# A two-block transformer kernel on one core: rotary step, scores and softmax of an attention stage reordered among three engines

## The chip, the cores and the metric

The kernel runs on one core of one Trainium2 chip. The time is device time in microseconds of one execution; lower is better. TensorE (PE) multiplies, VectorE (DVE) and ScalarE (ACT) do the elementwise work, SyncE (SP) issues the loads of the weights.

## What is computed

A sequence of 256 tokens of width 1024 in float32 passes through a first block of two layers and then a second block. The change lies in the token mixer of the second block alone. Cut to what matters there:

```python
def causal_depthwise_conv(u, w, b): ...      # 31 taps, 1024 channels

def mla_attention(q_nope, q_rope, k_nope, k_rope, v):
    sc = (einsum("bqhd,bkhd->bhqk", qn_b, k_nope)            # 128 deep
          + einsum("bqhr,bkr->bhqk", qr_b, k_rope)) * scale  # 64 deep, one key part for all 8 heads
    sc = where(causal, sc, -1e30)
    p = softmax(sc, axis=-1)
    return einsum("bhqk,bkhd->bqhd", p, v)

z = h @ w_in
u = silu(layer_norm(causal_depthwise_conv(ua * sigmoid(ub), conv_w, conv_b)))
y_a = u @ w_conv_out
q = rms_norm(q_lat) @ w_uq                # 8 heads of 128 + 64
kv = rms_norm(kv_lat) @ w_ukv             # 8 heads of 128 + 128
q_rope, k_rope = apply_rope(...), apply_rope(...)
y_b = mla_attention(q_nope, q_rope, k_nope, k_rope, v) @ w_attn_out
return (g_a * y_a + g_b * y_b) @ w_out
```

## The kernel before, in words

Each engine has a program of its own, written out by hand, and the programs meet at semaphores. Tokens are two tiles of 128 (`NT`), channels are eight tiles of 128 (`KT`).

A large matrix product is done in three: a value is held as a rounded high part (`wh`, `xh`) and a remainder (`wl`, `xl`), and PE multiplies high by high, low by high and high by low (lines 668 to 670). So each block of weights that SP has loaded into `raw` is split: ACT copies it into `wh` (line 1608), then DVE subtracts it from `raw` into `wl` (line 2300). `raw`, `wh` and `wl` have three slots each, and the blocks take them in a rotation that `make_plan` fixes. `split_hi` on ACT waits until PE has used the slot's last block (`w_used`), `split_lo` on DVE waits until ACT has written the slot (`hi_ready`). Both engines run their instructions in program order, so a split that waits holds up what stands behind it. The order of blocks at this place is `uq` 0 to 3, `ukv` 0 and 1, `attn_out` (0,0), (0,1), (1,0), (1,1), then `conv_out` and `out`. `ukv` 0 and 1 lie in slots 1 and 2, `attn_out` (0,0), (0,1), (1,0) in slots 0, 1, 2, and `attn_out` (1,1) in slot 0 again.

The stages around the change, in the order of PE's program:

- `uq` and `ukv`: the queries (`qn`), the keys (`kn`) and the values (`vt`) of eight heads; ACT takes them out of PSUM. `ukv` comes as two blocks of four heads, each first the keys, then the values.
- Rotation: DVE rotates the 64-wide parts of queries and key into `ro` (lines 3042 to 3048, semaphore `roped`). PE transposes `ro` in ten pieces (line 878 is the helper `turn`), ACT writes them to `qr`.
- Attention, one head after another (`scores`, lines 1510 and 1511, and `weigh`). For a head, PE makes the scores of two token tiles, of 128 and of 256 keys, each as a product 128 deep and one 64 deep in the upper or lower half of the rows. DVE scales and masks them (lines 3073 to 3075), takes the maxima (3079) and negates them (3081). ACT does the exponentials (2199, with the sums). DVE divides (`finish`, 3058 and 3061). PE transposes the weights, ACT copies them (`weights_T`, 2187), PE multiplies them with the values (1538 to 1540), ACT and DVE take the result apart into `xh` (`out_hi`, 2191) and `xl` (`out_lo`, 3066).
- The depthwise convolution fills the gaps of this. DVE does 217 taps of seven channel tiles (line 2971, `conv(n)` runs the next n of them), some before, some inside and the last 16 after the heads. PE does the 31 taps of the eighth tile, four for each head (`conv_taps`, line 1522), with diagonal matrices that ACT builds (`diag_taps`, line 2178) in two buffers.
- `attn_out`: four blocks, each 24 products for two token tiles. After the first of them PE makes the convolution's mean (`conv_mean`, line 1563), which needs all taps of DVE; after the second its variance (`conv_var`, line 1570). From the variance a chain through DVE and ACT (lines 3101 to 3121) makes the input of `conv_out`, the next stage of PE.

Of the kernel before, what the change touches and what calls it, by code (L numbers as in the profile page):

```python
# [21 lines left out]
ALU = mybir.AluOpType  # L22
# [41 lines left out]
MASKS = (("causal", P), ("unit", CH), ("diag_ts", CH), ("off_ts", CH), ("diag_st", CH), ("strict_st", CH), ("upto_st", CH), ("incl_st", P))  # L64
# [10 lines left out]
def constants():  # L75
# [15 lines left out]
    out = np.zeros((P, NMASK), np.float32)  # L91
    for n, v in m.items():
        out[:, MI[n]:MI[n] + v.shape[1]] = v
# [39 lines left out]
    "pe_18": (("ffn0.out", 3), ("ffn1.out", 3), ("out.t", 1), ("mlp.out", 3)),  # L133
# [64 lines left out]
    "dve_24": (("scaled", 16), ("at.max", 8)),  # L198
# [98 lines left out]
def build(nc, A, masks_d, pool_d, out):  # L297
    plan = make_plan()
    ctx = ExitStack()
    with ctx:  # L300
# [365 lines left out]
        def _(pe):  # L666
# [797 lines left out]

            for j in range(2):
# [6 lines left out]
                for i in range(4):  # L1472
                    for kt in range(2):
                        mm3(ps[:, bk + i // 2, (i % 2) * SEQ:(i % 2 + 1) * SEQ], w4[0][:, kt, i, 0:NOPE], w4[1][:, kt, i, 0:NOPE],
                            xh[:, 3 + kt, :], xl[:, 3 + kt, :], kt == 0, kt == 1)
# [5 lines left out]

            ro = W(3, 0, 1280).rearrange("p (t n) -> p t n", t=NT)
            pe.wait_ge(S("roped"), B("roped") + 2)
            pe.wait_ge(S("kn"), B("kn") + 2)
            pe.wait_ge(S("vt"), B("vt") + 2)
            for kt in range(5):
                b = 4 + kt // 2
                for t in range(NT):
                    m = turn(ps[:, b, (kt % 2) * SEQ + t * P:(kt % 2) * SEQ + (t + 1) * P], ro[:, t, kt * P:(kt + 1) * P])
                if kt in (1, 3, 4):  # L1490
                    m.then_inc(S("ro_T"), 1)
# [9 lines left out]
            pe.wait_ge(S("vt"), B("vt") + 4)  # L1501

            def scores(i):
                if i >= 2:
                    pe.wait_ge(S("at.sc"), B("at.sc") + 2 * (i - 1))
                rows = slice(64 * (i % 2), 64 * (i % 2) + 64)
# [7 lines left out]
            diags = DIAGS(W, lowr)  # L1514
# [10 lines left out]
            def weigh(i):  # L1525
# [7 lines left out]
                conv_taps(i)  # L1533
# [8 lines left out]
            scores(0)  # L1542
            for i in range(NH):
                if i + 1 < NH:
                    scores(i + 1)
                weigh(i)
# [26 lines left out]
            linear("attn_out", "at.xl", 2, free=ao_free, after={(0, 0): conv_mean, (0, 1): conv_var})  # L1573
# [20 lines left out]
        def _(act):  # L1594
# [556 lines left out]
            for j in range(2):  # L2151
                used(act, ("ukv", j))
                for b in range(2):
                    act.activation(kn[:, 4 * j + 2 * b:4 * j + 2 * b + 2, :], ps[:, UKV_BANK[j] + b, :].rearrange("p (a n) -> p a n", a=2), ACT.Copy)\
                       .then_inc(S("kn"), 1)
                vt = W3(5, NT)
                for t in range(NT):
                    act.activation(vt[:, t, j * 512:(j + 1) * 512], ps[:, UKV_BANK[j] + 2 + t, :], ACT.Copy).then_inc(S("vt"), 1)
                if j == 0:
                    split(("attn_out", 0, 0), ("attn_out", 0, 1))  # L2160
# [31 lines left out]
            for i in range(NH):  # L2192
                b = i % 2
                if i:
                    weights_T(i - 1)
# [1185 lines left out]
```

## Time and profile before

| | |
|---|---|
| median of 3 runs | 1197.58 us (1197.08 to 1199.15) |
| the profiled execution | 1196.4 us, of which its span 1194.3 us |
| PE busy | 1136.8 us (95%) |
| DVE busy | 825.4 us (69%) |
| ACT busy | 558.4 us (47%) |
| chain that ended last | PE 68%, DVE 21%, ACT 6%, issue 3%, DMA 2% |

PE is busy in nearly all of the span, so this is a kernel whose time is PE's own work and the places where PE waits or runs at the lower clock. The whole attention stage takes some 45 us of the span, from 870 to 915 us.

### The profile page before, as it was taken

Reading aid. Unit: us, or ns where it says so; the run is one execution under the profiler, and the core shown is the slowest. Engines: PE = TensorE matmul, PEld = TensorE weight load, DVE = VectorE, ACT = ScalarE, POOL = GpSimd, SP = SyncE. Lnnn points to the kernel's source line nnn. Section 1 sums busy time; section 2 is a strip of 40 time slices with the busy share of each in tenths; the row PEclk is TensorE's granted clock in tenths of the full one; section 3 lists DMA queues with packets and bytes.
Section 4 is the critical chain, followed back from the end, with each engine's and each line's share of the span. In section 5 each row is a group of like instructions: output and inputs, shape, how many; then the busy total and the mean of one; then the engine's idle time right before and its main releaser. Section 6 shows DMA issues by size and latency. Waiting matters only on the chain.

```text
span 1194.3 us, 20769 instructions
## 1 busy us (share of the span) xinstructions
PE 1136.8 (95%) x8520; PEld 959.7 (80%) x8520; DVE 825.4 (69%) x1173; ACT 558.4 (47%) x708; POOL 42.0 (4%) x48
## 2 busy tenths in 40 slices
PE   8999999999999887989999999999999999999998
PEld 7887888889688586767877787877967878999996
DVE  3555444558398476859999986998998667455554
ACT  5535643354654634344343464354464646344443
POOL 0000000000001400101111000000000000000000
PEclk9999999999999999989999999999989999999999
DMA  9385555652333110879999954464520344455532
GB/s 316 111 272 198 169 178 208 211 176 106 106 106 112 49 29 22 307 240 320 328 328 333 306 176 141 132 199 128 176 106 2 122 160 146 171 177 174 195 122 106
DMA packets 129476, 207.96 MB, mean 174 GB/s; under 512 B 11192, under 2 KB 86717, under 8 KB 129150
## 3 DMA queue, kind: packets, MB, share of 16 engines
q1 hardware_dynamic: 121716, 176.58, 44.6%
q0 software_dynamic: 6672, 27.26, 6.6%
q10 hardware_dynamic: 1018, 3.10, 0.7%
q8 instruction: 53, 0.87, 0.3%
q14 instruction: 17, 0.14, 0.0%
HBM read 204.83 MB, written 1.05 MB: 172 GB/s over the span
## 4 chain that ended last, share of the span: by engine, by line
PE 68%; DVE 21%; ACT 6%; issue 3%; DMA 2%; ACTq 0%; DVEq 0%; SPq 0%
PE ps L668 19%; PE ps L670 19%; PE ps L669 18%; DVE wl L2300 6%; DVE wide L2971 3%; PE ps L1061 2%; ACT wh L1608 2%; DVE wide L2410 2%; DMA raw<-in_ffn_w_up 1%; PE ps L745 1%; PE ps L878 1%; PE ps L974 1%; ACT wide L2199 1%; PE ps L1093 1%; PE ps L1366 1%
## 5 line engine op out<-in xcount | busy, mean ns | idle before, releaser
L2300 DVE TENSOR_TENSOR wl<-raw,wh 128x2048 fp32r<-128x2048 f32 (+3 forms) x158 | 354.2, 2248 | 157.8 <-ACT wh L1608 157.5
L668 PE MATMUL ps<-wh,xh 128*128 128x512 f32 (+4 forms) x1128 | 417.2, 370 | 12.8 <-DVE wl L2300 3.9
L670 PE MATMUL ps<-wl,xh 128*128 128x512 f32 (+4 forms) x1128 | 408.9, 363 | 0.0
L669 PE MATMUL ps<-wh,xl 128*128 128x512 f32 (+4 forms) x1128 | 408.4, 362 | 0.0
L1608 ACT ACTIVATE wh<-raw 128x2048 fp32r<-128x2048 f32 (+3 forms) x158 | 294.1, 1881 | 92.0 <-PE ps L670 79.8
L668 PEld LDWEIGHTS ps<-wh,xh 128*128 128x128 f32 x1128 | 213.9, 190 | 53.4 <-issue 12.4
L670 PEld LDWEIGHTS ps<-wl,xh 128*128 128x128 f32 x1128 | 213.5, 189 | 33.0
L669 PEld LDWEIGHTS ps<-wh,xl 128*128 128x128 f32 x1128 | 213.9, 190 | 31.5 <-issue 0.7
L668 PE MATMUL ps<-wh,gh 128*128 128x512 f32 x280 | 109.6, 391 | 1.9 <-DVE gl L2473 1.9
L669 PE MATMUL ps<-wh,gl 128*128 128x512 f32 x280 | 109.1, 390 | 0.0
L670 PE MATMUL ps<-wl,gh 128*128 128x512 f32 x280 | 109.0, 389 | 0.0
L1703 ACT ACTIVATE gh<-ps 128x512 fp32r<-128x512 f32 x20 | 12.0, 599 | 161.4 <-PE ps L745 161.4
L2971 DVE SCALAR_TENSOR_TENSOR wide<-wide,cols 128x256 f32<-128x256 f32 x210 | 86.3, 477 | 0.0
L2410 DVE SCALAR_TENSOR_TENSOR wide<-wide,small 128x256 f32<-128x256 f32 x192 | 78.4, 478 | 0.0
L668 PEld LDWEIGHTS ps<-wh,gh 128*128 128x128 f32 x280 | 52.6, 188 | 12.8 <-DVE gl L2473 2.1
L670 PEld LDWEIGHTS ps<-wl,gh 128*128 128x128 f32 x280 | 52.6, 188 | 11.1
L669 PEld LDWEIGHTS ps<-wh,gl 128*128 128x128 f32 x280 | 52.6, 188 | 10.3
L2436 DVE TENSOR_TENSOR gl<-ps,gh 128x512 fp32r<-128x512 f32 x20 | 13.8, 692 | 63.2 <-ACT gh L1703 62.3
L878 PE MATMUL ps<-masks,wide 128*128 128x128 f32 (+1 forms) x194 | 26.7, 277 | 6.4 <-DVE wide L3133 2.0
L878 PEld LDWEIGHTS ps<-masks,wide 128*128 128x128 f32 (+1 forms) x194 | 21.4, 140 | 12.5 <-issue 3.8
L2462 DVE TENSOR_TENSOR wide<-wide 128x512 f32<-128x512 f32 x16 | 11.1, 692 | 28.8 <-ACT wide L1730 28.8
L621 POOL DMA_DIRECT2D wide<-in_w_ada x24 | 21.3, 891 | 227.5 <-DVE wide L2410 163.1
(377 smaller groups left out, 1173.3 us busy)
## 6 DMA issues: line engine op xcount, KB each, us to landing
wide<-in_w_ada POOLq DMA_DIRECT2D x24, 1024.0 KB, 9.1
raw<-in_ffn_w_gate SPq DMA_DIRECT2D x44, 512.0 KB, 4.2
raw<-in_ffn_w_up SPq DMA_DIRECT2D x44, 512.0 KB, 5.3
raw<-in_ffn_w_down SPq DMA_DIRECT2D x22, 1024.0 KB, 5.1
raw<-in_w_mlp_in SPq DMA_DIRECT2D x16, 1024.0 KB, 7.0
raw<-in_w_mlp_out SPq DMA_DIRECT2D x16, 1024.0 KB, 5.2
raw<-in_w_in SPq DMA_DIRECT2D x16, 512.0 KB, 4.9
raw<-in_w_in SPq DMA_DIRECT2D x8, 1024.0 KB, 5.1
```

What stands on the lines that cost most here:

```text
L621: pool.dma_start(ada_raw[2 * (j % 2) + b], ada_src[:, :, n0:n0 + 256])\
L668: pe.matmul(o, lh, rh, start=start, stop=False)
L669: pe.matmul(o, ll, rh, start=False, stop=False)
L670: return pe.matmul(o, lh, rl, start=False, stop=stop)
L878: return pe.transpose(dst, src, masks[0:nk, 0:nk])
L1061: m = pe.matmul(bank(g, b + half)[to, at + j * w:at + (j + 1) * w], T(g, l, p, e, q), T(g, r, p, e, q, w), start=True, stop=True)
L1608: act.activation(wh[:, s, 0:width], raw[:, s, 0:width], ACT.Copy).then_inc(hi_ready[s], 1)
L1703: act.activation((xh if last else gh)[:, 0:2, :], ps[:, 6, :].rearrange("p (a n) -> p a n", a=2), ACT.Copy).then_inc(S(f + ".gh"), 1)
L2300: v.tensor_tensor(wl[:, s, 0:width], raw[:, s, 0:width], f32(wh[:, s, 0:width]), ALU.subtract).then_inc(lo_ready[s], 1)
L2410: v.scalar_tensor_tensor(out=o, in0=ada_raw[buf][:, k, :], scalar=ccol[:, k:k + 1], in1=o, op0=ALU.mult, op1=ALU.add).then_inc(S("ada_step ...
L2436: v.tensor_tensor(lo[:, 0:2, :], ps[:, 6, :].rearrange("p (a n) -> p a n", a=2), f32(hi[:, 0:2, :]), ALU.subtract)\
L2971: m = v.scalar_tensor_tensor(out=cv[:, kt, :], in0=src, scalar=w, in1=cv[:, kt, :], op0=ALU.mult, op1=ALU.add)
```

## The change

1. The rotation comes earlier. DVE no longer does nine taps ahead of the split of `ukv` 1. PE transposes the rotated parts between the keys and the values of `ukv` 1 instead of after the values, ACT writes `kn` and `qr` first and `vt` after, and loads the table of the exponential before them. ACT's first `diag_taps` stands ahead of `vt`.
2. Scores of two heads are made together: both heads' products 128 deep, then both heads' products 64 deep, one in each half of the rows, into two banks of PSUM. `weigh` of an even head issues the next pair's scores, and the taps of PE run one head ahead.
3. Scale, mask and maximum are one `tensor_tensor_reduce` for each token tile, on the negated scores: two instructions of DVE for a head in place of six. The exponential has a scale of -1.
4. DVE takes two heads per turn of its loop (`scored`, `conv(3)`, `scored`, `out_lo`, `conv(2)`, `finish`, `conv(4)`, `finish`, `conv(2)`, `out_lo`). The splits of `attn_out` (0,0), (0,1), (1,0), two of which stood ahead of the heads, close the first three turns. The split of (1,1), which stood behind the last tap, now stands ahead of the last 11 taps and of the last `out_lo`. Splits on ACT stand at the same places, save that of (1,1), which stays behind `conv_pe`.
5. `attn_out` is written out: (0,0) needs only four heads of `xl`; `conv_mean` stands in the middle of (0,1) and `conv_var` in the middle of (1,0).

```diff
+            def scores(j):
+
+                if j:
+                    pe.wait_ge(S("at.sc"), B("at.sc") + 4 * j)
                 for t in range(NT):
                     nk = P * (t + 1)
-                    o = ps[:, i % 2, t * SEQ:t * SEQ + nk]
-                    pe.matmul(o, qn[:, i, tok(t)], kn[:, i, 0:nk], start=True, stop=False)
-                    m = pe.matmul(o, qr[rows, i // 2, tok(t)], qr[rows, 4, 0:nk], start=False, stop=True)
-                m.then_inc(S("at.s"), 1)
+                    o = [ps[:, e, t * SEQ:t * SEQ + nk] for e in range(2)]
+                    for e in range(2):
+                        pe.matmul(o[e], qn[:, 2 * j + e, tok(t)], kn[:, 2 * j + e, 0:nk], start=True, stop=False)
+                    for e in range(2):
+                        rows = slice(64 * e, 64 * e + 64)
+                        m = pe.matmul(o[e], qr[rows, j, tok(t)], qr[rows, 4, 0:nk], start=False, stop=True)
+                        if t == NT - 1:
+                            m.then_inc(S("at.s"), 1)
...
-                conv_taps(i)
+                if i % 2 == 0 and i + 2 < NH:
+                    scores(i // 2 + 1)
+                if i + 1 < NH:
+                    conv_taps(i + 1)
...
-            linear("attn_out", "at.xl", 2, free=ao_free, after={(0, 0): conv_mean, (0, 1): conv_var})
+            ao_free(0)
+            for c in range(2):
+                o = [ps[:, 2 * c + t, :] for t in range(NT)]
+                s = arrive(("attn_out", c, 0))
+                if c == 0:
+                    pe.wait_ge(S("at.xl"), B("at.xl") + 4)
+                half(s, range(0, 2), o, 512, True, False)
+                if c:
+                    conv_var()
+                half(s, range(2, 4), o, 512, False, False, 2).then_inc(w_used[s], 1)
+                s = arrive(("attn_out", c, 1))
+                if c == 0:
+                    pe.wait_ge(S("at.xl"), B("at.xl") + NH)
+                half(s, range(4, 6), o, 512, False, False)
+                if c == 0:
+                    conv_mean()
+                half(s, range(6, 8), o, 512, False, True, 2).then_inc(w_used[s], 1)
...
+            for j in range(2):
+                if j == 0:
+                    used(act, ("ukv", 0))
+                else:
+                    act.activation(unused, eps, ACT.Exp)
+                    act.wait_ge(S("ukv.k"), B("ukv.k") + 1)
...
+            for i in range(0, NH, 2):
+                exps(i)
+                if i:
+                    out_hi(i - 2)
+                    weights_T(i - 1)
+                exps(i + 1)
+                diag_taps(i + 1)
+                if i:
+                    out_hi(i - 1)
+                weights_T(i)
+                if i + 2 < NH:
+                    diag_taps(i + 2)
+                    split(("attn_out",) + AO_AT[i])
+            out_hi(NH - 2)
             weights_T(NH - 1)
             out_hi(NH - 1)
             act.wait_ge(S("conv_mm"), B("conv_mm") + NH)
...
-            for name in [("uq", 3), ("ukv", 0), ("ukv", 1)]:
-                conv(9)
+            for name, n in [(("uq", 3), 9), (("ukv", 0), 9), (("ukv", 1), 0)]:
+                conv(n)
                 split(name)
...
-            split(("attn_out", 0, 0), ("attn_out", 0, 1))
-            conv(10)
+            conv(19)
...
-                v.scalar_tensor_tensor(out=pp[b][:, 0, 0:P], in0=ps[:, b, 0:P], scalar=SCALE, in1=causal, op0=ALU.mult, op1=ALU.add)
-                v.tensor_scalar(pp[b][:, 1, 0:P], ps[:, b, SEQ:SEQ + P], SCALE, None, ALU.mult).then_inc(S("at.sc"), 1)
-                v.scalar_tensor_tensor(out=pp[b][:, 1, P:SEQ], in0=ps[:, b, SEQ + P:2 * SEQ], scalar=SCALE, in1=causal, op0=ALU.mult,
-                                       op1=ALU.add).then_inc(S("at.sc"), 1)
-                v.wait_ge(S("at.sc"), B("at.sc") + 2 * (i + 1))
                 for t in range(NT):
-                    m = v.tensor_reduce(amax[:, 2 * b + t:2 * b + t + 1], pp[b][:, t, 0:P * (t + 1)], AX_X, ALU.max)
-                link(m)
-                v.tensor_scalar(amax[:, 2 * b:2 * b + 2], amax[:, 2 * b:2 * b + 2], -1.0, None, ALU.mult).then_inc(S("at.max"), 1)
+                    nk = P * (t + 1)
+                    v.tensor_tensor_reduce(out=pp[b][:, t, 0:nk], in0=ps[:, b, t * SEQ:t * SEQ + nk], in1=causal[t], scale=-SCALE, scalar=3e38,
+                                           op0=ALU.add, op1=ALU.min, accum_out=amax[:, 2 * b + t:2 * b + t + 1]).then_inc(S("at.sc"), 1)
+
+            for i in range(0, NH, 2):
+                scored(i)
+                conv(3)
+                scored(i + 1)
+                if i:
+                    out_lo(i - 2)
                 conv(2)
                 finish(i)
-                if i == 1:
-                    split(("attn_out", 1, 0))
-                conv(2 if i == 1 else 3)
+                conv(4)
+                finish(i + 1)
+                conv(2)
                 if i:
                     out_lo(i - 1)
+                if i in AO_AT:
+                    split(("attn_out",) + AO_AT[i])
+            out_lo(NH - 2)
+            split(("attn_out", 1, 1))
+            conv(3)
             out_lo(NH - 1)
             conv(len(taps))
-            split(("attn_out", 1, 1))
...
+AO_AT = {0: (0, 0), 2: (0, 1), 4: (1, 0)}
```

## Rows read from the trace of the kernel before

**Rows 1.** PE timeline, four places: start us, us, line, count, idle before.
```profile
519.06 1.33 PE L722 MATMUL ps<-masks,h 128*128 128x128 f32 x5 [5.26 <-DVE h L2393]
...
854.19 0.38 PE L668 MATMUL ps<-xh,wh 128*128 128x256 f32 x1 [1.38 <-DVE wl L2300]
...
867.05 1.25 PE L878 MATMUL ps<-masks,wide 128*128 128x128 f32 x10
870.63 0.49 PE L1510 MATMUL ps<-wide 128*128 128x128 f32 x2 [2.32 <-ACT wide L2165]
```

**Rows 2.** Windows: engines' busy us and instructions, then granted PE clock, DMA share, GB/s.
```profile
520.00:524.00 4.00, 4.00 (x13) 3.32 (x12) 2.87 (x6) 2.82 (x8) 0.00 (x0) 0.50 1.07 383
...
872.50:882.70 10.20, 9.72 (x28) 6.70 (x27) 9.45 (x30) 6.90 (x19) 0.00 (x0) 0.50 0.25 93
```

**Rows 3.** PE timeline, one head of the steady loop.
```profile
889.41 0.55 PE L878 MATMUL ps<-masks,wide 128*128 128x128 f32 x3
889.79 1.89 PE L1522 MATMUL ps<-wide 128*128 128x256 f32 x8
891.52 0.38 PE L1538 MATMUL ps<-wide 128*128 128x128 f32 x2
...
892.19 0.39 PE L1510 MATMUL ps<-wide 128*128 128x128 f32 x2
...
894.17 0.55 PE L878 MATMUL ps<-masks,wide 128*128 128x128 f32 x3
```

**Rows 4.** DVE timeline, the same head.
```profile
889.67 0.28 DVE L3073 SCALAR_TENSOR_TENSOR wide<-ps,masks 128x128 f32<-128x128 f32 x1
...
891.11 0.87 DVE L2971 SCALAR_TENSOR_TENSOR wide<-wide,cols 128x256 f32<-128x256 f32 x2
892.25 0.17 DVE L3058 RECIPROCAL small<-small 128x2 f32<-128x2 f32 x1 [0.27 <-ACT wide L2199]
...
892.92 1.27 DVE L2971 SCALAR_TENSOR_TENSOR wide<-wide,cols 128x256 f32<-128x256 f32 x3
894.11 0.41 DVE L3066 TENSOR_TENSOR xl<-ps,xh 128x256 fp32r<-128x256 f32 x1
```

**Rows 5.** DVE timeline, the same kind of instruction as the new one, elsewhere.
```profile
793.36 0.42 DVE L2308 CUSTOM_DVE_ANT_0 wide<-wide 128x256 f32<-128x256 f32 x1
...
793.71 0.55 DVE L2308 CUSTOM_DVE_ANT_0 wide<-wide 128x384 f32<-128x384 f32 x1
```

**Rows 6.** DVE timeline, ahead of the heads.
```profile
854.06 3.64 DVE L2971 SCALAR_TENSOR_TENSOR wide<-wide,cols 128x256 f32<-128x256 f32 x9
...
865.52 4.49 DVE L2300 TENSOR_TENSOR wl<-raw,wh 128x2048 fp32r<-128x2048 f32 x2 [0.17 <-ACT wh L1608]
```

**Rows 7.** ACT timeline, one head of the steady loop.
```profile
891.23 0.40 ACT L2199 ACTIVATE wide<-wide,small 128x128 f32<-128x128 f32 x1 [0.75 <-DVE small L3081]
...
892.12 1.26 ACT L2178 ACTIVATE wide<-masks,cols 128x128 f32<-128x128 f32 x4
...
894.76 0.49 ACT L2187 ACTIVATE wide<-ps 128x384 f32<-128x384 f32 x1 [1.10 <-PE ps L878]
```

**Rows 8.** PE timeline behind the heads: `attn_out`, `conv_mean`, `conv_var`, start of `conv_out`.
```profile
914.38 0.48 PE L668 MATMUL ps<-wh,xh 128*128 128x512 f32 x1
...
919.92 3.96 PE L1563 MATMUL ps<-wide,ones 128*128 128x256 f32 x16
...
929.22 3.62 PE L1570 MATMUL ps<-wide,ones 128*128 128x256 f32 x16
...
944.06 0.47 PE L668 MATMUL ps<-wh,xh 128*128 128x512 f32 x1 [0.31 <-DVE xl L3121]
```

**Rows 9.** Timelines of ACT (first row) and DVE behind the heads.
```profile
920.18 1.91 ACT L1608 ACTIVATE wh<-raw 128x2048 fp32r<-128x2048 f32 x1 [4.77 <-PE ps L670]
...
922.12 2.29 DVE L2300 TENSOR_TENSOR wl<-raw,wh 128x2048 fp32r<-128x2048 f32 x1 [0.28 <-ACT wh L1608]
...
933.63 0.42 DVE L3101 TENSOR_SCALAR lowr<-ps 128x256 f32<-128x256 f32 x1
```

More of the change, by code:

```diff
@@ L132 @@
     "pe_12": (("cum", 1), ("conv_mm", 8)),
-    "pe_18": (("ffn0.out", 3), ("ffn1.out", 3), ("out.t", 1), ("mlp.out", 3)),
+    "pe_18": (("ffn0.out", 3), ("ffn1.out", 3), ("ukv.k", 1), ("out.t", 1), ("mlp.out", 3)),
     "pe_13": (("rk_T", 1), ("pc_T", 1), ("at.o", 8)),
@@ L1463, in _, with rope_transposes @@
                 m.then_inc(w_used[s], 1)
+            ro = W(3, 0, 1280).rearrange("p (t n) -> p t n", t=NT)
+            def rope_transposes():
+                pe.wait_ge(S("roped"), B("roped") + 2)
+                pe.wait_ge(S("kn"), B("kn") + 2)
+                pe.wait_ge(S("vt"), B("vt") + 2)
+                for kt in range(5):
+                    b = 4 + kt // 2
+                    for t in range(NT):
+                        m = turn(ps[:, b, (kt % 2) * SEQ + t * P:(kt % 2) * SEQ + (t + 1) * P], ro[:, t, kt * P:(kt + 1) * P])
+                    if kt in (1, 3, 4):
+                        m.then_inc(S("ro_T"), 1)
             for j in range(2):
@@ L1542, in _ @@
             scores(0)
+            conv_taps(0)
+            pe.wait_ge(S("vt"), B("vt") + 4)
             for i in range(NH):
-                if i + 1 < NH:
-                    scores(i + 1)
                 weigh(i)
@@ L2178, in diag_taps @@
                     act.activation(d, ident, ACT.Copy, scale=cols[:, c:c + 1]).then_inc(S("diag"), 1)
-            diag_taps(0)
+            for j in range(2):
[4 more added lines that the diff above has]
+                    act.wait_ge(S("ukv.k"), B("ukv.k") + 1)
+                for b in range(2):
+                    act.activation(kn[:, 4 * j + 2 * b:4 * j + 2 * b + 2, :], ps[:, UKV_BANK[j] + b, :].rearrange("p (a n) -> p a n", a=2), ACT.Copy)\
+                       .then_inc(S("kn"), 1)
+                if j:
+                    for b in range(3):
+                        n = 2 if b < 2 else 1
+                        act.wait_ge(S("ro_T"), B("ro_T") + b + 1)
+                        act.activation(qr[:, 2 * b:2 * b + n, :], ps[:, 4 + b, 0:n * SEQ].rearrange("p (a n) -> p a n", a=n), ACT.Copy)\
+                           .then_inc(S("ro_put"), 1)
+                    act.wait_ge(S("glu"), B("glu") + 8)
+                    act.wait_ge(S("roped"), B("roped") + 2)
+                    diag_taps(0)
+                    used(act, ("ukv", 1))
+                vt = W3(5, NT)
+                for t in range(NT):
+                    act.activation(vt[:, t, j * 512:(j + 1) * 512], ps[:, UKV_BANK[j] + 2 + t, :], ACT.Copy).then_inc(S("vt"), 1)
             pp = [W3(10, NT, 512 * b, 512) for b in range(2)]
@@ L3048, in _ @@
                 v.tensor_copy(ro[:, t, 576:640], ro[:, t, 512:576]).then_inc(S("roped"), 1)
-            split(("attn_out", 0, 0), ("attn_out", 0, 1))
-            conv(10)
+            conv(19)
             pp = [W3(10, NT, 512 * b, 512) for b in range(2)]
-            causal = masks[:, MI["causal"]:MI["causal"] + P]
+            causal = [masks[:, MI["causal"] - P * t:MI["causal"] + P] for t in range(NT)]
             def finish(i):
@@ L3066, in out_lo, with scored @@
                 v.tensor_tensor(xl[:, i, :], ps[:, 4 + i % 2, 0:SEQ], f32(xh[:, i, :]), ALU.subtract).then_inc(S("at.xl"), 1)
-            for i in range(NH):
+            def scored(i):
                 b = i % 2
@@ L3256, in CONV_OUT, with DIAGS @@
     return ps[:, 6 + b, o * SEQ:(o + 1) * SEQ]
-def DIAGS(W, lowr):
-    one = [W(3, o, P) for o in range(0, TAP_BATCH * P, P)]
-    return one, [W(8, o, P) for o in range(0, 1024, P)] + [lowr[:, 512 + o:512 + o + P] for o in range(0, 512, P)]
+def DIAGS(W):
+    return [W(8, o, P) for o in range(0, TAP_BATCH * P, P)], [W(3, o, P) for o in range(0, TAP_BATCH * P, P)]
+AO_AT = {0: (0, 0), 2: (0, 1), 4: (1, 0)}
 def ADA_AT(n):
```

60 lines of the change are left out of this document (13 added, 47 removed).

## The prediction

> **What bounds the kernel now.** I read the page first: PE is busy in nearly every slice, so time is lost only where PE waits or runs at half clock. Then I read the PE timeline of the attention stage for its idle times and the windows for its clock. PE waits 2.32 us for the rotated queries before the first scores [rows 1], and soon after runs 10.2 us at a granted clock of 0.50, 1.2 of its 2.4 GHz [rows 2]. Then comes a steady loop of one head in 4.77 us (889.41 to 894.17), without a gap on PE [rows 3]: transposes 0.38, four taps 1.73, value products 0.67, scores 1.98. DVE needs the same 4.77 us, with 0.27 idle: scaling to negated maximum 1.44, taps 0.40 each, `finish` 0.67, `out_lo` 0.33 [rows 4]. So in the loop PE and DVE are level, and neither alone would shorten it. Behind the loop PE starts `attn_out` at 914.38, ends its first block at 919.92, makes `conv_mean`, starts `conv_var` at 929.22 and `conv_out` at 944.06 [rows 8]. Two chains cross there. The split of `attn_out` (1,1): ACT had waited 4.77 us for the end of `attn_out` (0,0) before it wrote the high part, and DVE followed at 922.12, 2.2 us after that end [rows 9]. And the taps of DVE, which end just ahead of that split, and which `conv_mean` needs. From 944.06 on the program is unchanged and PE is the bound, so I count the change in the start of `conv_out`.
>
> **The change part by part.**
>
> *Rotation.* DVE did nine taps (3.56 us) ahead of the split of `ukv` 1 and ended the rotation where the next split began its wait, at 865.35 [rows 6]; now it ends at 861.8. PE reaches the transposes at the end of the keys, and the values follow; both together still end at 868.3 (867.05 and 1.25) [rows 1]. ACT writes keys and `qr` meanwhile, so scores start at 868.3, not at 870.63: 2.3 us gained. `vt` lands about 1.3 us after the scores start, ahead of the first value products, and costs nothing. DVE does its 19 taps by 869.4.
>
> *Scores.* 1.98 us for a head [rows 3]. A transpose and a value product of the same 128 columns take 0.13 and 0.22, a tap of 256 columns 0.43, so the columns of a head cost 1.3 and the changes between 128 and 64 rows 0.7. The pair has the columns of two and the changes of one: 2.6 + 0.7 = 3.3. Ends: 3.96 if nothing is saved, 2.65 if the two halves run at once. I take 3.3. Above it nothing decides, as DVE is later in the loop (below).
> First the row, then a rule. The scores cost 0.7 more than their columns [rows 3]. The Trainium skill, TensorEngine Tiling (Array Packing), Key Properties, says that a change of tiling mode drains the engine, with which this agrees, and that different tiles can multiply in parallel, which no row here shows. By it the pair would take 2.65, and the sum below would start 0.6 earlier and give 1203.1.
>
> *The new instruction.* No row has it on PSUM. The same custom instruction on 256 SBUF columns steps by 0.35 (793.36 to 793.71) [rows 5]; 128 columns I put at 0.22, so `scored` costs 0.57 instead of 1.44. Bounds: 0.5, if 128 columns step like the plain 0.20 of the old loop's instructions and nothing is added by PSUM, and 0.84, if both take the full 0.42 of the first row. 0.87 saved for a head, 7 us of DVE in all. But it lies beside PE in the loop.
>
> *The loop.* For a turn of two heads DVE now has 2 x 0.57, 11 taps of 0.40, 2 x 0.67, 2 x 0.33 = 7.5 us, and in three turns a split of 2.2: 9.7. PE has 0.76 + 3.3 + 3.46 + 1.34 = 8.9. ACT per turn: exponentials 2 x 0.9, diagonals 2 x 1.2, the copy of 0.5 twice [rows 7], `out_hi` 2 x 0.3, high split 1.9: 7.7, but strung between waits. Following the queues: DVE waits for the first pair's scores until 871.3, reaches the first split at 878.2, and ACT, which must first do exponentials, two sets of diagonals and a copy, has the high part at 879.1: a wait of 1.0. The next two splits wait 0.8 each by the same count. First turn 10.0 us (no `out_lo` in it), second and third 10.5 each. The last turn reaches the end of the last `finish` after 6.3 us, at 908.7. PE is idle 1.5 to 1.9 us per turn. Then transposes, copy and value products of the last head, 1.6 us: `attn_out` starts at 910.3 instead of 914.38. So far 4.1 us are gained.
>
> *The split of (1,1).* Here the gain goes. DVE comes to it at 910.2. It needs ACT's high part, which needs `w_used` of slot 0, that is the end of `attn_out` (0,0). That block takes 5.54 us (914.38 to 919.92) [rows 8], so it ends at 915.8, and DVE may start 2.2 later [rows 9], at 918.0. DVE stands still for 7.8 us with 11 taps and the last `out_lo` queued behind. In the kernel before only the split itself waited, with all taps done. Then split 2.2, three taps, `out_lo`: 921.7. PE needs that `out_lo` for `attn_out` (0,1) and waits from 915.8 to 921.9, 6.1 us. The last eight taps end at 924.9. Without anything of the clock PE does the first 12 products of (0,1) by 924.6, then `conv_mean`, whose first channel tiles cover the last taps, by 928.3, then 24 products (5.45) to 933.7.
>
> *The clock.* After 5.26 us of idle PE ran a following window wholly at 0.50 and came back at about 5.1 us after its start [rows 1, 2]. The new idle time is 6.1, so I take the same 5.1 us at half speed, which costs half: 2.4. `conv_var` then starts at 936.1, against 929.22: +6.9. Of this 0.7 comes back: the variance's first step on DVE at 933.63 stood behind a split [rows 9], which is done in time now. From there the chain of DVE and ACT is unchanged; PE has 8.2 us of `attn_out` behind `conv_var` in place of 10.9, less than the chain of 10.4 us, so `conv_out` starts with the chain.
>
> **Sum.** +6.9 - 0.7 = +6.2 on `conv_out`, say 6.1. The profiled execution took 1196.4 us, so 1202.5; the median of the three runs lies 1.2 above it, so 1203.7.
>
> **The rivals.**
> 1. *The clock falls inside the loop too.* For it: it fell after idles of 1.38 and 2.32 us [rows 1], and the low stretch of rows 2 lasted 10.2 us through scores and taps. The new loop has 1.5 to 1.9 idle per turn. At half clock the pair's scores take 6.6 us and taps 3.5, and DVE's second `scored` of a turn, which needs PE's transposes of the head before, is held for some 2 to 4 us per fall. One fall: `conv_out` at +8 to +10, 1205.7 to 1207.7. Also of this kind: PE idles 2.6 us ahead of `conv_out`; a fall there costs 1.6. Against it: in each turn PE is fuller than in the stretch that fell.
> 2. *Not slower measurably.* The splits in the loop don't wait (2.6 less) and the clock costs nothing (2.4 less): +1.1, 1198.7.
> 3. *Faster: the queue behind the split of (1,1) doesn't stand still.* If slot 0 were free when DVE comes to it, split, three taps, `out_lo` and eight taps would end at 917.3, PE would run through from 910.3, `conv_var` would start at 927.6 and `conv_out` 2.3 us early: 1195.3, and 1194.7 with the pair's scores at their lower end. It decides only where the split's wait is under about 3 us. Against it: `make_plan` gives (1,1) the slot of (0,0), and rows 9 show ACT in just that wait.
> 4. *The change doesn't do what it says*: the new instruction is dear on PSUM, or the rotation still ends late. Rotation late by 2 us means +8.
>
> **How the numbers follow.** About 0.2% (2.4 us) is what a measurement of this kernel can tell from no change. Chances: forecast mechanism without a fall of the clock in the loop 0.47; with one (rival 1) and the late cases of rival 4 0.33; rival 2 0.12; rival 3 0.08, of which 0.06 beyond the bound. The range goes from rival 2 to the upper end of rival 1 with the second fall added, 1198.6 to 1209.3; it leaves out rival 3, and what lies above. Faster 0.06, within 0.2% 0.14, slower 0.80. The forecast's own range is 1201 to 1206: the ends of the pair's scores (0.6 either way), the price of `scored` (0.2 x 8 halved, as waits take part of it), and the clock between 0 and 2.4.
>
> **What would show it.** Right: scores start near 868.3 without the 2.32 idle; two custom instructions for a head, near 0.22 and 0.35; `attn_out` starts before 914; then a wait of DVE's line of splits for ACT of some 8 us, the longest of the stage, a wait of PE of about 6 us for `xl` in the middle of `attn_out`, and a granted clock of 0.5 after it; `conv_var` after 933. Wrong: DVE passes that split with a wait under 3 us, or the turns take under 9 us, or PE's idle time in the turns is gone because the clock fell and PE became the bound.

## The result, and the profile after

| | before | after |
|---|---|---|
| median, runs side by side | 1199.15 us (1195.91 to 1204.84, 7 runs) | 1207.58 us (1204.15 to 1212.92, 7 runs) |
| ratio of the times | | 1.0078, 95% interval 1.0056 to 1.0100 |
| profiled execution, span | 1196.4, 1194.3 us | 1212.92, 1210.9 us |
| PE, DVE, ACT busy | 1136.8, 825.4, 558.4 us | 1140.7, 818.6, 557.3 us |
| chain: PE, DVE, ACT | 68%, 21%, 6% | 71%, 18%, 5% |

The change made the kernel slower by 0.56 to 1.0%, some 7 to 12 us. DVE has 7 us less to do, as planned; the time is lost elsewhere.

The two profiled executions differ by 16.5 us, and half of that isn't the change. `ukv` 0, ahead of everything that was changed, already starts at 862.62 instead of 854.19 [rows 1], 8.43 us late. One stretch shows why: after, then before, the same 20 us of the span (engines' busy us and instructions, granted clock, DMA share, GB/s). A granted clock of 1.00 is TensorE's full speed of 2.4 GHz, 0.50 is half of it.

```profile
400.00:420.00 20.00, 17.52 (x395) 10.48 (x394) 4.75 (x7) 7.97 (x11) 9.43 (x8) 0.70 0.09 29
```

```profile
400.00:420.00 20.00, 16.49 (x519) 12.30 (x510) 8.23 (x12) 12.80 (x16) 12.73 (x11) 1.00 0.18 44
```

The granted clock was 0.70 where the kernel before had 1.00, on code that is the same in both, which is up to 6.0 us of PE's time. The 50 us ahead of it have 0.95 against 1.00, up to another 2.5; together that is the size of the 8.43. A second profile of the changed kernel (below) reaches `ukv` 0 at 854.40. So I compare the stage by distances, or by times of after minus 8.43. First PE, from the rotation's transposes to `conv_out`; columns as in rows 1.

```profile
872.65 1.25 PE L879 MATMUL ps<-masks,wide 128*128 128x128 f32 x10
...
876.48 0.60 PE L1516 MATMUL ps<-wide 128*128 128x128 f32 x4
877.02 0.49 PE L1519 MATMUL ps<-wide 64*128 64x128 f32 x4
877.44 1.13 PE L1516 MATMUL ps<-wide 128*128 128x256 f32 x4
878.50 0.70 PE L1519 MATMUL ps<-wide 64*128 64x256 f32 x4
879.13 1.99 PE L1531 MATMUL ps<-wide 128*128 128x256 f32 x8
883.22 0.52 PE L879 MATMUL ps<-masks,wide 128*128 128x128 f32 x3 [2.09 <-DVE wide L3100]
...
918.81 0.47 PE L669 MATMUL ps<-wh,xh 128*128 128x512 f32 x1
...
930.53 0.77 PE L669 MATMUL ps<-wh,xh 128*128 128x512 f32 x1 [6.00 <-DVE xl L3105]
...
935.05 3.61 PE L1575 MATMUL ps<-wide,ones 128*128 128x256 f32 x16
...
943.97 3.62 PE L1582 MATMUL ps<-wide,ones 128*128 128x256 f32 x16
...
958.05 0.75 PE L669 MATMUL ps<-wh,xh 128*128 128x512 f32 x1 [2.28 <-DVE xl L3166]
```

Less 8.43, the scores start at 868.05 without the wait of rows 1, `attn_out` starts at 910.38 instead of 914.38 [rows 8], PE then stands 6.00 us in the middle of its first half, and `conv_var` starts at 935.54 instead of 929.22. `conv_out`, the start of what wasn't changed, comes at 949.62 instead of 944.06: 5.6 us late. The first row behind the 6.00 lasts 0.77 where the same product otherwise lasts 0.47: half clock. The same is seen at `conv_out`, 0.75 behind an idle of 2.28.

DVE and, last row, ACT at the same place:

```profile
912.77 0.42 DVE L3105 TENSOR_TENSOR xl<-ps,xh 128x256 fp32r<-128x256 f32 x1
...
917.58 0.75 DVE L3105 TENSOR_TENSOR xl<-ps,xh 128x256 fp32r<-128x256 f32 x2
926.58 2.29 DVE L2340 TENSOR_TENSOR wl<-raw,wh 128x2048 fp32r<-128x2048 f32 x1 [8.24 <-ACT wh L1636]
...
929.97 0.42 DVE L3105 TENSOR_TENSOR xl<-ps,xh 128x256 fp32r<-128x256 f32 x1
```

```profile
924.63 1.91 ACT L1636 ACTIVATE wh<-raw 128x2048 fp32r<-128x2048 f32 x1 [4.80 <-PE ps L671]
```

This is the stall of the change. DVE wants to split `attn_out` (1,1) and stands still for 8.24 us, until ACT, which itself waits 4.80 us for PE to release the slot, has written the high part. Behind the split stand three taps and the last `out_lo` (929.97), and PE's row at 930.53 waits for just that. In the kernel before, the same wait on DVE was 0.28 us, with nothing urgent behind it [rows 9].

The clock in the windows behind the two idles of PE:

```profile
930.20:933.60 3.40, 3.07 (x7) 2.48 (x8) 3.35 (x9) 0.00 (x0) 0.00 (x0) 0.50 0.80 295
...
958.00:961.40 3.40, 3.35 (x8) 2.70 (x9) 3.08 (x2) 3.13 (x2) 0.00 (x0) 0.51 0.01 2
```

They are at 0.50 and 0.51, that is the lower level, 1.2 of 2.4 GHz. The 1.6 below is read from the next transposes: they stand 23.48 us behind the start of `conv_out`, against 21.89 before. The stage's loss is 5.6 us ahead of `conv_out` and 1.6 behind it, 7.2 in all.

### The profile page after: what moved, and what is told of

Same layout as the page of the kernel before. It is cut to its first block, busy times and chain, and to the rows that moved or that the text cites. A ratio compares the mean times of both kernels' runs of the same rounds, so it can differ in the third digit from the quotient of the medians.

```text
span 1210.9 us, 20755 instructions
## 1 busy us (share of the span) xinstructions
PE 1140.7 (94%) x8520; PEld 961.3 (79%) x8520; DVE 818.6 (68%) x1157; ACT 557.3 (46%) x709; POOL 42.0 (3%) x48
## 3 DMA queue, kind: packets, MB, share of 16 engines
HBM read 204.90 MB, written 1.05 MB: 170 GB/s over the span
## 4 chain that ended last, share of the span: by engine, by line
PE 71%; DVE 18%; ACT 5%; issue 3%; DMA 2%; ACTq 0%; DVEq 0%; SPq 0%
PE ps L669 19%; PE ps L671 19%; PE ps L670 19%; DVE wl L2340 6%; DVE wide L3011 2%; ACT wh L1636 2%; PE ps L1062 2%; PE ps L879 2%; DVE wide L2450 1%; DMA raw<-in_ffn_w_up 1%; PE ps L746 1%; PE ps L975 1%; PE ps L1094 1%; PE ps L1367 1%; PE ps L974 1%
```

## The experiments

My theory: the loss is the split of (1,1) in front of the taps and of `out_lo`, 8 us of standing still on DVE that reach PE as 6 us of idle time plus a fall of the clock; the rest of the change gains. Rivals: the order of `attn_out`, `conv_mean` and `conv_var` itself costs; the pair of scores and the two-head turn cost; the clock alone costs, whatever DVE does. Each experiment ran beside the kernel before. I name distances from the start of `attn_out` (after: `conv_var` at +25.16, `conv_out` at +39.24; before: +14.84 and +29.68) and from the ten transposes of the rotation to `attn_out` (after: 46.16).

**The split alone moved back** (from the changed kernel).

```diff
             out_lo(NH - 2)
-            split(("attn_out", 1, 1))
             conv(3)
             out_lo(NH - 1)
             conv(len(taps))
+            split(("attn_out", 1, 1))
```

> The changed kernel with one edit: on DVE the split of attn_out (1,1) stands behind the last tap again, as in the kernel before. Theory (that split's wait for the end of attn_out (0,0) holds up 11 taps and the last out_lo): DVE's last out_lo comes about 8 us sooner, PE's 6 us wait in the middle of attn_out is gone and with it the half clock behind it; conv_var starts 17.2 us after attn_out does instead of 25.2, conv_out starts 8 us sooner in the stage, and the whole is 2 us faster than the kernel before (ratio 0.998), 8 to 9 us faster than the changed one. Rival (the loss lies in the loop of the heads or in the order of mean and variance): less than 3 us of the loss comes back, ratio 1.005 or more.

Measured: median 1196.89 us against 1197.90 of before, ratio 1.0006 (0.9986 to 1.0026). DVE, then PE:

```profile
910.46 0.42 DVE L3105 TENSOR_TENSOR xl<-ps,xh 128x256 fp32r<-128x256 f32 x1
910.80 3.25 DVE L3011 SCALAR_TENSOR_TENSOR wide<-wide,cols 128x256 f32<-128x256 f32 x8
...
917.50 2.29 DVE L2340 TENSOR_TENSOR wl<-raw,wh 128x2048 fp32r<-128x2048 f32 x1 [3.46 <-ACT wh L1636]
```

```profile
918.01 3.62 PE L1575 MATMUL ps<-wide,ones 128*128 128x256 f32 x16
...
926.94 3.62 PE L1582 MATMUL ps<-wide,ones 128*128 128x256 f32 x16
...
941.02 0.47 PE L669 MATMUL ps<-wh,xh 128*128 128x512 f32 x1 [2.27 <-DVE xl L3166]
```

One line moved and PE's idle time of 6.00 us is gone: `conv_var` stands at +17.18 instead of +25.16, `conv_out` at +31.26 instead of +39.24, 8.0 us earlier. The time follows: the ratio falls from 1.0078 to 1.0006, some 8.6 us. I had expected 0.998, which the interval leaves just outside; the fall of the clock shown below was not in it. DVE still waits 3.46 us for ACT, but nobody waits for what is behind. That settles the largest part. It leaves a kernel that isn't faster than before, although `attn_out` starts some 4 us earlier in it. Of these, 1.6 go up to `conv_out` (+31.26 against +29.68), which the last row shows with 2.27 us of idle ahead of it, and about as much in the low clock behind it:

```profile
942.00:946.00 4.00, 4.00 (x12) 3.11 (x11) 3.68 (x5) 2.09 (x2) 0.00 (x0) 0.57 0.03 1
```

**The old order of `attn_out` as well.** The same kernel, with part 5 of the change taken back too.

```diff
-            ao_free(0)
-            for c in range(2):
...
-                half(s, range(6, 8), o, 512, False, True, 2).then_inc(w_used[s], 1)
+            linear("attn_out", "at.xl", 2, free=ao_free, after={(0, 0): conv_mean, (0, 1): conv_var})
```

> As e1_split_last, and attn_out in the order of the kernel before: mean behind block (0,0), variance behind (0,1). With the split out of the way the taps of DVE end before attn_out (0,0) does, so conv_mean can start 5.5 us after attn_out and nothing waits. Theory: conv_var starts 14.8 us after attn_out as in the kernel before, 2.5 us sooner than in e1_split_last, PE's idle time ahead of conv_out shrinks from about 2.3 us to under 0.5; 4 to 5 us faster than the kernel before, ratio 0.996, if no clock fall is saved besides. Rival (the mean in the middle of the block is what pays): slower than e1_split_last.

Measured: 1193.58 us, ratio 0.9971 (0.9952 to 0.9990). `conv_mean` at +5.56, `conv_var` at +14.49, `conv_out` at +29.33 with an idle of 0.31 and no fall of the clock. The expected 0.996 lies in the interval:

```profile
938.19 0.47 PE L669 MATMUL ps<-wh,xh 128*128 128x512 f32 x1 [0.31 <-DVE xl L3150]
```

So the written-out order costs 1.9 us up to `conv_out` (31.26 to 29.33) and 1.6 for the clock behind it. The variance stands in the middle of `attn_out` (1,0), later than in the old order, and has too little of PE's work behind it to cover the chain through DVE and ACT. What is left of the change, with the loop of two heads and the earlier rotation in it, makes the kernel 0.3% faster.

**The new instruction alone**, put into the kernel before.

```diff
-                v.scalar_tensor_tensor(out=pp[b][:, 0, 0:P], in0=ps[:, b, 0:P], scalar=SCALE, in1=causal, op0=ALU.mult, op1=ALU.add)
...
-                v.tensor_scalar(amax[:, 2 * b:2 * b + 2], amax[:, 2 * b:2 * b + 2], -1.0, None, ALU.mult).then_inc(S("at.max"), 1)
+                for t in range(NT):
+                    nk = P * (t + 1)
+                    v.tensor_tensor_reduce(out=pp[b][:, t, 0:nk], in0=ps[:, b, t * SEQ:t * SEQ + nk], in1=causal[t], scale=-SCALE, scalar=3e38,
+                                           op0=ALU.add, op1=ALU.min, accum_out=amax[:, 2 * b + t:2 * b + t + 1]).then_inc(S("at.sc"), 1)
```

> The kernel before with the fused scale, mask and minimum on DVE alone. Theory (PE and DVE are level at 4.77 us for a head): DVE's busy time for a head falls by 0.85 us, but the heads still come every 4.7 to 4.8 us because PE is full; gain under 1 us in the stage, ratio 0.999 to 1.001. Rival (DVE alone bounds the loop): heads every 4.0 us, 5 to 6 us faster, ratio 0.995.

Measured: 1195.76 us, ratio 0.9983 (0.9963 to 1.0003): the interval holds no change. PE, then DVE, in its loop:

```profile
885.38 0.55 PE L878 MATMUL ps<-masks,wide 128*128 128x128 f32 x3
...
890.15 0.55 PE L878 MATMUL ps<-masks,wide 128*128 128x128 f32 x3
```

```profile
890.25 0.29 DVE L3075 CUSTOM_DVE_ANT_0 wide<-ps,masks 128x128 f32<-128x128 f32 x1 [0.38 <-PE ps L1511]
```

A head still takes 4.77 us on PE, as in rows 3, and DVE now waits for PE. The old loop was bound by both; freeing one of them moves nothing inside it. From the start of `ukv` 0 to `attn_out` this profile has 57.70 us against 60.19, of which 1.4 is a fall of the clock at `ukv` 0 that only the profile of before has; the rest comes at the loop's two ends.

**The scores of the pair in the old order of products**: each product 64 deep right behind the one 128 deep.

```diff
                     for e in range(2):
                         pe.matmul(o[e], qn[:, 2 * j + e, tok(t)], kn[:, 2 * j + e, 0:nk], start=True, stop=False)
-                    for e in range(2):
                         rows = slice(64 * e, 64 * e + 64)
```

> The changed kernel with the scores of two heads still issued together, but each head's product 64 deep right behind its product 128 deep, so that the two row halves never stand side by side and the row mode changes twice as often. Theory: a pair costs 3.96 us instead of 2.65, but PE has 1.8 us of idle time in each turn of two heads, so only the first pair, which DVE waits for, is late: attn_out starts 0.7 to 1.3 us later in the stage, and the time is 1 us over that of the changed kernel. Rival (PE bounds the loop): 4 x 1.3 = 5 us later.

Measured: 1204.64 us (4 runs), ratio 1.0053 (1.0034 to 1.0073), not to be told from the changed kernel.

```profile
867.90 0.38 PE L1516 MATMUL ps<-wide 128*128 128x128 f32 x2
...
871.97 1.99 PE L1530 MATMUL ps<-wide 128*128 128x256 f32 x8
```

The two heads' scores take 4.07 us (867.90 to 871.97) instead of 2.65 (876.48 to 879.13 above), so the pairing saves 1.4 us of PE for a pair. In the steady turns PE's idle time falls from 0.88 + 0.93 to 0.65 and the turn stays 10.5 us (transposes at +21.20, +31.70 and +42.20): DVE sets it, and what the pairing saves there PE spends waiting. At the first pair it brings 0.16 us: DVE starts on the first head's scores 6.75 us behind the transposes instead of 6.59, as it waits for that head alone, and in this order of products its head is done first. `attn_out` comes at 46.31 instead of 46.16, 0.15 later where I had expected 0.7 to 1.3. The rival in which the pair is what costs is out. Nor is the turn of two heads a loss: with it, and all else ahead of `attn_out`, that starts 4.0 us earlier than before.

**PE kept at work through the wait**, to part the idle time from the clock. 48 products whose results nobody uses stand ahead of the wait for the last `out_lo`.

```diff
                 if c == 0:
+                    spin(6, 48)
                     pe.wait_ge(S("at.xl"), B("at.xl") + NH)
```

> The changed kernel with 48 products of the identity with itself, some 5.9 us of PE work into a bank of PSUM that nobody reads, put where PE waits for the last out_lo inside attn_out. The chain of DVE is untouched, so only the clock can differ. Theory: no half clock behind the wait; conv_var starts 23.3 to 23.5 us after attn_out instead of 25.2; 1.8 us faster than the changed kernel, still 4 us or more slower than the kernel before. Rival (the idle time is the whole loss and the clock is nothing): no difference to the changed kernel.

```profile
917.76 10.88 PE L679 MATMUL ps<-masks 128*128 128x128 f32 x96
```

Measured: 1208.07 us, ratio 1.0084 (1.0062 to 1.0106). I had sized it wrongly: a filler takes 0.23 us (10.88 / 48; the trace has two rows for each), so they held PE 4.6 us longer than the wait would have. The run says nothing of the clock's share. Again, with 26:

> As e5_filled_wait, with 26 of the filling products instead of 48. There each took 0.22 us, not the 0.12 I had counted, so that PE was held 4.6 us beyond the last out_lo and nothing could be read from the time. 26 take 5.8 us, which ends as the wait does. Theory: granted clock 1.00 behind the wait, conv_var 23.2 to 23.5 us after attn_out (25.2 in the changed kernel), 1.8 us faster than the changed kernel on the same chip. Rival (the clock costs nothing that DVE's chain doesn't cost anyway): 25 us.

```profile
914.33 5.97 PE L679 MATMUL ps<-masks 128*128 128x128 f32 x52
...
932.20 3.62 PE L1582 MATMUL ps<-wide,ones 128*128 128x256 f32 x16
```

```profile
921.00:925.00 4.00, 4.00 (x20) 3.37 (x19) 2.51 (x7) 0.00 (x0) 0.00 (x0) 1.00 0.56 219
```

Measured: 1203.24 us, ratio 1.0048 (1.0031 to 1.0065). The fillers last as long as the wait, 5.97 us, the clock stays at 1.00 behind them, and `conv_var` comes at +23.41 instead of +25.16. So the clock's share of the loss is 1.8 us in these profiles, and the 6.0 of waiting stay whatever PE does in them. The medians point the same way (1203.24 against 1205.53 for the changed kernel beside it), though the intervals overlap. The clock alone isn't the cause.

**`out_lo` ahead of the split, taps behind it**, to part the two things that were queued.

```diff
             out_lo(NH - 2)
-            split(("attn_out", 1, 1))
             conv(3)
             out_lo(NH - 1)
+            split(("attn_out", 1, 1))
             conv(len(taps))
```

> The changed kernel with the split of (1,1) moved behind the next three taps and the last out_lo, but still ahead of the last eight taps. It separates what the stalled split holds up: the out_lo that PE wants for attn_out (0,1), and the taps that conv_mean wants. Theory: PE goes through to conv_mean and then waits there for the last taps, which end about 13 us after attn_out starts; conv_var starts 20.4 us after attn_out, up to 22.2 if the clock falls in that wait (25.2 in the changed kernel, 17.2 in e1_split_last). Rival (out_lo is all that matters): 17.2 to 17.7.

Measured: 1199.64 us, ratio 1.0024 (1.0009 to 1.0039). DVE waits at the split as before, PE now inside `conv_mean`:

```profile
917.15 2.29 DVE L2340 TENSOR_TENSOR wl<-raw,wh 128x2048 fp32r<-128x2048 f32 x1 [6.63 <-ACT wh L1636]
```

```profile
922.66 1.99 PE L1575 MATMUL ps<-wide,ones 128*128 128x256 f32 x8 [3.11 <-DVE wide L3011]
```

`conv_var` stands at +20.56. Of the 8.0 us between the changed kernel and the first experiment, 4.6 go when `out_lo` and its three taps leave their place behind the split (25.16 to 20.56), and 3.4 when the eight taps leave it too (20.56 to 17.18). The clock's 1.8 us are in the 4.6: behind the wait of 3.11 the clock stayed at 1.00. The eight taps behind the split are enough to make the kernel slower than before. A kernel with `out_lo` alone behind it was not run, so what that would cost by itself is not shown.

**ACT's splits inside the heads ahead of its diagonals**, on top of the second experiment.

```diff
                 if i + 2 < NH:
-                    diag_taps(i + 2)
                     split(("attn_out",) + AO_AT[i])
+                    diag_taps(i + 2)
```

> e2_mean_first, with ACT's high split in each turn ahead of its second set of diagonals instead of behind it. DVE's waits of 1.16, 0.76 and 0.76 us ahead of its three splits go; the diagonals come 1.9 us later, but PE needs them only after the scores and four taps of the head before. Theory: DVE bounds the loop, so attn_out starts 2.4 to 2.7 us sooner in the stage and the time falls by as much; 6 to 7 us under the kernel before, ratio 0.994 to 0.995. Rival (PE or ACT is level with DVE): under 1 us.

Measured: 1190.70 us (1188.69 to 1191.91, 6 runs) against 1196.75, ratio 0.9942 (0.9925 to 0.9960). DVE at the splits of the three turns, which waited 1.16, 0.76 and 0.76 us in the changed kernel; the first there, then the first two here:

```profile
887.26 2.29 DVE L2340 TENSOR_TENSOR wl<-raw,wh 128x2048 fp32r<-128x2048 f32 x1 [1.16 <-ACT wh L1636]
```

```profile
877.84 2.29 DVE L2324 TENSOR_TENSOR wl<-raw,wh 128x2048 fp32r<-128x2048 f32 x1 [0.28 <-ACT wh L1620]
...
888.10 2.28 DVE L2324 TENSOR_TENSOR wl<-raw,wh 128x2048 fp32r<-128x2048 f32 x1
```

The waits are down to 0.28, nothing and nothing, and `attn_out` comes 44.16 us behind the transposes instead of 46.16. So 2.40 us of waits are gone and 2.00 are gained, a little less than the 2.4 to 2.7 that I expected. In this profile the clock fell in the first turn, and DVE waits 0.52 us for PE's transposes there, which it did not in the changed kernel. DVE sets the pace of the turns, so its waits are worth nearly their length. This version is faster than both kernels, by 0.6% beside the kernel before and, by the two ratios, by 1.4% against the changed one.

**The rotation alone**, put into the kernel before: DVE's nine taps behind the rotation, PE's transposes between keys and values, ACT's order as in the change; PE's wait for the values ahead of the scores is kept.

```diff
-            for name in [("uq", 3), ("ukv", 0), ("ukv", 1)]:
-                conv(9)
+            for name, n in [(("uq", 3), 9), (("ukv", 0), 9), (("ukv", 1), 0)]:
+                conv(n)
                 split(name)
...
+            conv(9)
             split(("attn_out", 0, 0), ("attn_out", 0, 1))
```

> The kernel before with the rotation alone moved: DVE does the nine taps behind the rotation instead of ahead of the split of ukv 1, PE transposes between keys and values, ACT writes keys and qr ahead of the last values; the two splits of attn_out and ten taps still stand ahead of the heads. My prediction counted 2.3 us for this step. Theory now: PE's scores start 1 us or more sooner, but DVE has the same work ahead of its first head and reaches it at the same time, so attn_out starts at the same time within 0.5 us (apart from what the clock does), and the 2.3 us need the splits moved as well; ratio 0.998 to 1.001. Rival (PE's late scores held the heads): 2 us or more faster.

Measured: 1197.72 us, ratio 1.0012 (1.0000 to 1.0024): no gain.

```profile
869.43 0.54 PE L1515 MATMUL ps<-wide 128*128 128x128 f32 x2 [3.49 <-ACT wide L2188]
```

```profile
870.00:874.00 4.00, 4.00 (x9) 2.25 (x10) 3.81 (x13) 0.58 (x1) 0.00 (x0) 0.50 0.98 370
```

With the values waited for ahead of the scores, PE is idle for 3.49 us instead of 2.32 and the clock is at 0.50 behind that. So the scores did not start 1 us sooner, as I had expected. They start 16.07 us behind `ukv` 0, against 16.44 in the kernel before, and the 16.44 hold a fall of the clock worth 1.4. But sooner scores alone would have brought little, as DVE shows at its first head, in the kernel before and then here:

```profile
869.93 4.04 DVE L2971 SCALAR_TENSOR_TENSOR wide<-wide,cols 128x256 f32<-128x256 f32 x10
873.89 0.28 DVE L3073 SCALAR_TENSOR_TENSOR wide<-ps,masks 128x128 f32<-128x128 f32 x1
```

```profile
873.03 0.29 DVE L3084 SCALAR_TENSOR_TENSOR wide<-ps,masks 128x128 f32<-128x128 f32 x1 [0.15 <-PE ps L1516]
```

In the kernel before, DVE comes to its first head from two splits and ten taps and doesn't wait for PE at all; with the rotation moved it waits 0.15 us. In the changed kernel the two splits are gone from there and DVE waits 1.50 us for the scores. So by these rows the 2.3 us need the splits moved as well. What scores without the wait for the values bring was not run by itself.

**The changed kernel once more**, beside the filler of 26 and the next one.

> The changed kernel as it is, beside the others on one chip. Every theory: ratio 1.006 to 1.009.

Measured: 1205.53 us, ratio 1.0072 (1.0043 to 1.0101). Windows of 4 us behind four idles of PE: of 1.39, 2.09, 6.00 and 2.27 us.

```profile
854.40:858.40 4.00, 4.00 (x29) 3.83 (x30) 3.93 (x8) 0.23 (x1) 0.00 (x0) 1.00 0.68 227
873.57:877.57 4.00, 4.00 (x17) 2.89 (x17) 2.84 (x9) 3.96 (x8) 0.00 (x0) 0.57 0.00 0
920.97:924.97 4.00, 4.00 (x10) 3.13 (x11) 3.01 (x8) 0.00 (x0) 0.00 (x0) 0.50 0.65 250
948.71:952.71 4.00, 4.00 (x11) 3.15 (x12) 3.68 (x3) 3.08 (x2) 0.00 (x0) 0.57 0.01 2
```

The ratio and the stage repeat (`conv_var` at +25.40, `conv_out` at +39.48). Here the clock does fall in the first turn of the loop (0.57), where the first profile of the same kernel had 1.00, and stays up at `ukv` 0, where that one had 0.59. The 8.43 us upstream are not there.

**The six old instructions in the fastest version**, in place of the new one, with the semaphores and the exponential's scale as they belong to them.

```diff
-                    v.tensor_tensor_reduce(out=pp[b][:, t, 0:nk], in0=ps[:, b, t * SEQ:t * SEQ + nk], in1=causal[t], scale=-SCALE, scalar=3e38,
-                                           op0=ALU.add, op1=ALU.min, accum_out=amax[:, 2 * b + t:2 * b + t + 1]).then_inc(S("at.sc"), 1)
+                    m = v.tensor_reduce(amax[:, 2 * b + t:2 * b + t + 1], pp[b][:, t, 0:P * (t + 1)], AX_X, ALU.max)
+                link(m)
+                v.tensor_scalar(amax[:, 2 * b:2 * b + 2], amax[:, 2 * b:2 * b + 2], -1.0, None, ALU.mult).then_inc(S("at.sc"), 2)
```

> e6_hi_earlier with the fused instruction undone: scale, mask, maxima and negation as in the kernel before, 1.44 us for a head instead of 0.57. Theory (DVE bounds the new loop, since the loop carries the splits): attn_out starts 8 x 0.87 = 7 us later in the stage, ratio back to 0.999 to 1.001; so the fused instruction, worth next to nothing in the old order (e3_fused_only), is worth 7 us in the new one. Rival (its worth is the same in both): 1 to 2 us.

Measured: 1199.65 us, ratio 1.0011 (0.9996 to 1.0026). `attn_out` comes 52.53 us behind the transposes instead of 44.16: 8.4 us, of which 8 x 0.89 = 7.1 is the instructions' own time; the other 1.3 were not taken apart. PE is idle for 4.00 us in the first turn and has a granted clock of 0.50 behind it:

```profile
877.43:881.43 4.00, 4.00 (x15) 3.11 (x15) 3.62 (x10) 3.69 (x9) 0.00 (x0) 0.50 0.00 0
```

In the two-head turn the new instruction is worth all it saves on DVE, and the time agrees: 1.0011 against 0.9942, each beside the kernel before, is some 8 us, 5.5 to 11 by the intervals. In the old loop it left no mark on the turn.

## Why the prediction was right, and where its terms were off

The direction, the mechanism and its place were as forecast, and the median of 1207.58 lies within the range, in its upper part. It lies above the forecast's own range of 1201 to 1206 and in the band of the first rival (1205.7 to 1207.7), but what that rival would cost isn't what put it there. The second fall of the clock did, with 1.6 us, and a base that was as much higher: the sum starts from 1197.58, and beside the changed kernel the kernel before took 1199.15. By the ratio the change costs 9.3 us, where 6.1 were forecast. Step by step, with times of after less 8.43:

- *Rotation.* Scores were put at 868.3 and start at 868.05. But this was costed as the rotation's own gain, and it isn't: in the kernel before, the same rotation gains nothing (1.0012), as DVE has its splits and taps to do until 873.89 there.
- *Scores of the pair.* This term was mis-sized: 3.3 taken, 2.65 measured, the lower end. In the rows of after the 64-deep products of two heads take 0.42 + 0.63 = 1.05 us, changes of depth included; their columns one after another would be half of 2 x 1.3, so 1.3. In the kernel before, those of one head alone take as long, 0.42 (892.50 to 892.92) and 0.62 (893.55 to 894.17, rows 3):

```profile
892.50 0.48 PE L1511 MATMUL ps<-wide 64*128 64x128 f32 x2
892.92 0.70 PE L1510 MATMUL ps<-wide 128*128 128x256 f32 x2
893.55 0.70 PE L1511 MATMUL ps<-wide 64*128 64x256 f32 x2
```

So the halves run at once. By this the rule of the Trainium skill (TensorEngine Tiling (Array Packing), Key Properties) on different tiles, which no row of before could show, agrees with the trace. But the 0.6 us that I had put on either end of this term aren't there: DVE waits for the first head only, and the whole pairing is worth 0.15 at `attn_out`.
- *The new instruction.* 0.57 forecast; the two step by 0.21 and 0.34 below, so 0.55.

```profile
879.24 0.29 DVE L3114 CUSTOM_DVE_ANT_0 wide<-ps,masks 128x128 f32<-128x128 f32 x1 [1.50 <-PE ps L1519]
879.45 0.42 DVE L3114 CUSTOM_DVE_ANT_0 wide<-ps,masks 128x256 f32<-128x256 f32 x1
879.79 1.27 DVE L3011 SCALAR_TENSOR_TENSOR wide<-wide,cols 128x256 f32<-128x256 f32 x3
```

- *The loop.* Turns of 10.0 and 10.5 forecast, 10.2 and 10.5 measured; waits at the splits 1.0, 0.8, 0.8 forecast, 1.16, 0.76, 0.76 measured; PE idle 0.88 + 0.93 a turn, in the forecast's 1.5 to 1.9. `attn_out` at 910.38 against 910.3.
- *The split of (1,1).* A wait of 7.8 us until 918.0 forecast, 8.24 until 918.15 measured; PE's wait 6.1 forecast, 6.00 measured. The first experiment shows that these are the loss and not only beside it.
- *The clock behind it.* 2.4 us forecast from the stretch behind an idle of 5.26 (half of its 5.1 us would be 2.55), 1.8 measured (+25.16 against +23.41 with the fillers). This is most of the difference between `conv_out` at +6.1, as forecast, and +5.6.
- *The second fall.* The step that was judged wrongly. The forecast saw the idle ahead of `conv_out` and left its clock in a rival, at 1.6 us, though it had the fall behind 2.32 us in its own rows. It happened in every one of the seven profiles with an idle of 2.27 or 2.28 there. With it the sum would have given 1203.7 + 1.6 = 1205.3. Measured, the stage loses 7.2 us.
- *The fall inside the loop* (the first rival) was put at 8 to 10 us in `conv_out`. It came in one of the two profiles of the changed kernel, behind the 2.09 of idle in the first turn. With it `attn_out` comes 46.23 us behind the transposes there, 46.43 with the split alone moved, and 47.49 both with 48 fillers and with `out_lo` ahead, against 46.15 to 46.16 in the three profiles of this loop without it: 0.1 to 1.3 us, where the forecast had at least 2. In each of these four it fell once and was over within the first turn, and held DVE up by no more than that.

What is left: the stage accounts for 7.2 us, and the two comparisons gave 1.0078 (9.3 us, 6.7 to 12) and 1.0072 (8.6 us, 5.1 to 12.1). The difference of 1 to 2 us lies within both intervals. It may be the clock in unchanged stages: behind the idle of 1.96 us further on, the profile of before has 1.00 and both profiles of the changed kernel have 0.61 to 0.63. But the kernels of experiments with no loss have either, so this was not shown to come from the change, and it stays open.

## What to carry over

When a step is moved forward in an engine's program, ask what releases it, and list what now stands behind it: here one subtraction of 2.3 us, which waited for another engine's release, held up the last input of the next product. A chain that must be covered wants its first step as early as the order allows, with the covering work behind it. An instruction made cheaper pays only where its engine sets the pace: the same fusion brought nothing that could be measured surely in one loop and 8 us in the other.

## What the runs showed of the chip

- The clock falls behind short idles of PE, and for some lengths only in some executions of the same code. In the 13 profiles, from `ukv` 0 to the start of `conv_out`, the granted clock of the 4 us behind an idle of 0.84 to 0.93 was 1.00 each time; behind 1.38 it was under 0.65 in six of 13, behind 2.09 in five of eight, behind 2.27 to 2.32 it was low in nine of nine (0.57 to 0.72), and so behind 3.49, 4.00 and 6.00 each time (0.50 to 0.56). Behind the 3.11 inside `conv_mean` of one experiment it stayed at 1.00. So length alone doesn't decide. I had not expected a choice for the very same idle in the very same code.
- Two products 64 deep in the two halves of the rows ran at once: those of two heads took 0.42 us (128 columns) and 0.63 (256 columns), as long as those of one head before, and the whole pair took 2.65 us in place of 4.07.
- Unchanged code upstream moved a profile by 8.4 us, and a lower granted clock upstream (0.70 for 20 us, 0.95 for the 50 ahead of them) is worth up to 8.5, so about all of it. A change of a few microseconds in a stage is read from distances within the stage, not from absolute times.
